# Six modulation units moved from TensorE to GpSimd, and the second block's first norm and latent products done tile by tile

## The reference, cut to what matters

```python
# first block
mod = (silu(c) @ w_mod[l] + b_mod[l])[:, None, :]              # 1024 x 6144
sh1, sc1, gt1, sh2, sc2, gt2 = jnp.split(mod, N_MOD, axis=-1)
h = layer_norm(x) * (1.0 + sc1) + sh1
y = hybrid_mixer(h, w_in, conv_w, ...)          # conv + chunked SSD, forgetting attention
x = layer_norm(ALPHA * x + (1.0 + gt1) * y, ln1_g, ln1_b)
h = layer_norm(x) * (1.0 + sc2) + sh2
y = hierarchical_moe(h, ...)                    # 16 experts, two of one group of four
x = layer_norm(ALPHA * x + (1.0 + gt2) * y, ln2_g, ln2_b)
# second block
mod = (silu(c_2) @ w_ada[l] + b_ada[l])[:, None, :]            # six more rows
h = rmsnorm(x, g_norm_mix) * (1.0 + sc1) + sh1
c_q, c_kv, k_pe, dil, gates = jnp.split(h @ w_in_2, ...)       # latents: the first 704 columns
o_a = mla_attention(...); o_b = three dilated attentions
x = x + gt1 * ((g_a * o_a + g_b * o_b) @ w_out)
x = x + gt2 * expert_choice_ffn(rmsnorm(x) * (1.0 + sc2) + sh2, ...)
```

## Time and profile before

| | |
|---|---|
| median of 3 runs | 2143.76 us (2142.66 to 2144.46) |
| the profiled execution | 2143.5 us |
| its span, first to last instruction | 2141.7 us |
| mean granted TensorE clock | 0.873 of full |
| busy: PE, PEld, DVE, ACT, POOL | 1616.5, 829.8, 419.9, 283.1, 60.3 us |
| read from HBM | 661.86 MB |

### The profile page before, as it was taken

The page is one execution under the profiler, slowest core; times in us unless marked ns, Lnnn a source line. Parts: engine busy times, 40 slices in busy tenths (PEclk is TensorE's granted clock), DMA queues, the critical chain, the costliest instruction groups (busy, mean ns, idle before and its releaser), DMA issues.

```text
span 2141.7 us, 19636 instructions
## 1 busy us (share of the span) xinstructions
PE 1616.5 (75%) x8021; PEld 829.8 (39%) x8021; DVE 419.9 (20%) x912; ACT 283.1 (13%) x632; POOL 60.3 (3%) x79
## 2 busy tenths in 40 slices
PE   6999999899998999999999644664365545545545
PEld 3774654344442677686644311311131111211111
DVE  5521642432213122121325200000000000000001
ACT  6211222110001222121233100000000000000000
POOL 2000000000000100111100000000000000000000
PEclk9999999989999999999999767877787777777777
DMA  9999332849997642344527499999999999999996
GB/s 354 336 365 348 105 100 79 343 164 421 427 428 293 225 176 100 133 143 138 175 75 287 197 428 428 428 427 429 427 428 427 428 427 428 427 428 428 427 428 265
DMA packets 104236, 670.53 MB, mean 313 GB/s; under 512 B 8227, under 2 KB 10984, under 8 KB 71120
## 3 DMA queue, kind: packets, MB, share of 16 engines
q1 hardware_dynamic: 100000, 657.63, 75.4%
q0 software_dynamic: 3712, 11.11, 1.6%
q10 hardware_dynamic: 432, 0.49, 0.1%
HBM read 661.86 MB, written 7.34 MB: 312 GB/s over the span
## 4 chain that ended last, share of the span: by engine, by line
PE 62%; DMA 32%; DVE 3%; ACT 2%; SPq 1%; issue 1%; DVEq 0%; ACTq 0%
PE psum L1099 14%; PE psum L1088 12%; DMA ring<-in_w_up 11%; DMA ring<-in_w_down 11%; PE psum L1695 10%; DMA ring<-in_w_gate 9%; PE psum L1434 5%; PE psum L1466 3%; PE psum L1351 2%; PE psum L1402 2%; PE psum L1054 2%; PE psum L1180 1%; PE psum L1473 1%; PE psum L1562 1%; SPq L786 1%
## 5 line engine op out<-in xcount | busy, mean ns | idle before, releaser
L1695 PE MATMUL psum<-work,prob 128*32 128x512 f32 x1024 | 290.9, 732 | 162.3 <-DMA ring<-in_w_up 87.2
L1695 PE MATMUL psum<-ring,prob 128*32 128x512 f32 x1024 | 291.0, 732 | 143.1 <-DMA work<-in_w_up 83.1
L1099 PE MATMUL psum<-ring,hT 128*128 128x512 f32 x672 | 306.3, 602 | 5.0 <-ACT hT L181 4.2
L1088 PE MATMUL psum<-hT,ring 128*128 128x256 f32 x1152 | 270.5, 381 | 1.6 <-ACT probT L181 0.8
L1088 PEld LDWEIGHTS psum<-hT,ring 128*128 128x128 f32 x1152 | 210.7, 190 | 36.2 <-issue 8.0
L1695 PE MATMUL psum<-work,hT 128*32 128x512 f32 x512 | 143.0, 721 | 82.7 <-DMA ring<-in_w_down 82.7
L1695 PE MATMUL psum<-ring,hT 128*32 128x512 f32 x512 | 143.0, 721 | 54.4 <-DMA work<-in_w_down 51.0
L1099 PEld LDWEIGHTS psum<-ring,hT 128*128 128x128 f32 x672 | 123.8, 193 | 138.6 <-issue 132.6
L1695 PEld LDWEIGHTS psum<-work,prob 128*32 128x32 f32 x1024 | 70.8, 131 | 267.2 <-issue 267.2
L1695 PEld LDWEIGHTS psum<-ring,prob 128*32 128x32 f32 x1024 | 71.0, 131 | 248.3 <-issue 247.3
L181 ACT ACTIVATE work<-psum 128x512 f32<-128x512 f32 (+2 forms) x99 | 57.0, 576 | 650.2 <-PE psum L1709 313.9
(11 more groups left out here) (334 smaller groups left out, 1430.0 us busy)
## 6 DMA issues: line engine op xcount, KB each, us to landing
work<-in_w_up SPq DMA_DIRECT2D x40, 2048.0 KB, 20.1
ring<-in_w_up SPq DMA_DIRECT2D x40, 2048.0 KB, 19.9
ring<-in_w_gate SPq DMA_DIRECT2D x38, 2048.0 KB, 18.8
work<-in_w_gate SPq DMA_DIRECT2D x38, 2048.0 KB, 19.6
work<-in_w_down SPq DMA_DIRECT2D x38, 2048.0 KB, 20.2
ring<-in_w_in SPq DMA_DIRECT2D x72, 1024.0 KB, 7.5
ring<-in_w_down SPq DMA_DIRECT2D x34, 2048.0 KB, 21.1
ring<-in_w_mod SPq DMA_DIRECT2D x24, 1024.0 KB, 12.5
```

Source lines behind the costliest of these rows:

```text
L1088: mm = pe.matmul(o[:, wide(j * S, S)], w[:, ch], actT[:, c, :], start=(c == 0), stop=(c == KC - 1))
L1099: mm = pe.matmul(o, lhs, w, start=(c == 0), stop=(c == KC - 1))
L1695: mm = pe.matmul(o[wide(i * CAP2, CAP2), :], lhs(chunks_per * piece + c, i), R.slot(l + i, (chunks_per, width))[:, c, wide(b * BANK, BANK) ...
```

## The change

Units 2 to 7 are no longer products on TensorE. POOL fetches their weights itself, 512 KB at a time (one channel chunk of one unit, 128x1024), multiplies each with the condition's value of that partition (tensor_scalar) and adds it to a running sum (tensor_tensor): 8 parts for each of 6 units. TensorE then only adds over the partitions, with a stationary block that has one column of ones (add_partitions: two products of 64 columns). The sums of unit 2 and 3 are taken behind the last xbc chunk and behind v, that of unit 4 in the SSD, those of 5, 6 and 7 in steps 2, 8 and 14 of the forgetting attention. Units 8 and 9 are still products; they stand behind z chunk 0 and z chunk 1.

Units 2 and 3 are spread after the first merge product and unit 4 after the last, and ACT takes them from PSUM. The register with the overflow flag is loaded before the rounds of experts. In the second block, each tile's first norm, modulation, transposes and latent products follow one another tile by tile; unit 8 is spread between the latents' transposes and q, and q_peT goes ahead of the second half of dil_q0's first chunk. One buffer of POOL's parts lies in h, three small tiles lose their own memory, and the constants get 32 columns.

```diff
-        IN_UNITS = dict(xbc=(2, 3, 4, 5), q=(6,), k=(7,), v=(8,), z=(9,))
+        IN_UNITS = dict(xbc={3: 2}, q={}, k={}, v={0: 3}, z={0: 8, 1: 9})
+        FOX_SUMS = {2: 5, 8: 6, 14: 7}
...
+        BESIDE_H = 3
+        part_places = [mod[:, 0, :], mod[:, 1, :], mod[:, 2, :], h[:, 0, :], h[:, 1, :], params[:, 1, :]]
+            streams = (2, 3, 4) if i < BESIDE_H else (2, 5)
...
+            def fetch_part(n):
+                u, c, b = unit_parts[n]
+                if c == 0 and u >= POOL_UNITS[2]:
+                    pool.wait_ge(*done(job(f"unit{u - 2}")))
+                if b == 5 and all(place != 5 for _, _, place in unit_parts[:n]):
+                    pool.wait_ge(bias_stored[BIAS_STAGES - 1], BIAS_GROUPS // BIAS_STAGES * BIAS_STORES)
+                if c and step.last:
+                    pool.wait_ge(*step.last)
+                src = (w_mod, w_ada)[u // 6].rearrange("(p c) n -> p c n", c=KC)[:, c, wide(u % 6 * D, D)]
+                pool.dma_start(part_places[b], src).then_inc(part_in[b], 16)
+
+            def add_part(n):
+                u, c, b = unit_parts[n]
+                pool.wait_ge(part_in[b], 16 * len([m for m in range(n + 1) if unit_parts[m][2] == b]))
+                step(nc.gpsimd.tensor_scalar, part_places[b], part_places[b], cact[:, u // 6, c:c + 1], None, ALU.mult)
+                if c:
+                    step(nc.gpsimd.tensor_tensor, unit_sum(u), part_places[b], unit_sum(u), ALU.add, signals=unit_summed(u) if c == KC - 1 else None)
+
+            def place_free(n, added):
+                u, c, b = unit_parts[n]
+                before = [m for m in range(n) if unit_parts[m][2] == b]
+                return n <= added + 6 and (c == 0 or not before or before[-1] <= added)
+
+            pool.wait_ge(signal("cact_ready"), 1)
+            pool.wait_ge(signal("hT_high"), KC // 2)
+            fetched = 0
+            for n in range(-1, len(unit_parts)):
+                if n >= 0:
+                    add_part(n)
+                while fetched < len(unit_parts) and place_free(fetched, n):
+                    fetch_part(fetched)
+                    fetched += 1
...
+            def add_partitions(u):
+                o = begin(job(f"unit{u}"))
+                pe.wait_ge(*unit_summed(u))
+                for n in range(2):
+                    mm = pe.matmul(o[wide(64 * n, 64), :], one_column_at(u), unit_sum(u)[:, wide(n * BANK, BANK)], start=True, stop=True)
+                units_done.append(u)
+                end(mm)
...
-            spread(2, 3, 4)
...
+            more_tokens = overflow_flag(pe)
...
-            with more_tokens(pe):
+            with pe.If(more_tokens > 0):
...
-            transpose_tokens("h3T", h, "h3_ready")
-            for k in range(4):
-                pe.wait_ge(*emptied(job("h3T", k)))
...
+            for t in range(TT):
+                transpose_tokens("h3T", h, "h3_ready", (t,))
+                if t:
+                    latent(1, 0)
+                for half in range(2):
+                    pe.wait_ge(*emptied(job("h3T", 2 * t + half)))
+                latent(0, t)
+            latent(1, 1)
...
+            spread(8)
             for k in range(4):
                 pe.wait_ge(*emptied(job("latT", k)))
...
-            in_one(channel_job("dil_q0", 0, 1, hT))
-            spread(8)
             for t in range(TT):
                 pe.wait_ge(signal("q_pe_ready"), t + 1)
...
+            in_one(channel_job("dil_q0", 0, 1, hT))
...
-                if ct % 4 == 3:
+                if ct % 4 == 3 and ct // 4 in IN_UNITS["xbc"]:
                     add_row(IN_UNITS["xbc"][ct // 4])
...
+            dve.wait_ge(*unit_summed(POOL_UNITS[BESIDE_H - 1]))
             for m in range(2 * TT):
                 assemble(m)
...
-            rms_modulated(0, "h3_ready")
+            dve.wait_ge(signal("params_in"), 64)
+            for t in range(TT):
+                norm_stats(6 + t, t, y_sum)
+                normalize(x, 6 + t, t, params[:, 0, :], params[:, 1, :], (signal("x_b1_ready"), t + 1), y_sum)
+                rms_modulated(0, "h3_ready", (t,))
```

## The result

The changed kernel takes 2183.78 us (median of 4 runs, 2180.33 to 2183.96) where the kernel before takes 2143.21: a ratio of 1.019, interval 1.0176 to 1.0205. It is 1.9% slower, clear of the noise, and the time lies above the range. The profiled execution has a span of 2178.5 us and a mean granted clock of 0.866.

A forecast was written before the change was run, and what follows sets the result against it. TensorE was taken to set the pace through the first block's experts, transfers from about 1200 us. Terms came to about 0 up to the experts, then -4.1 to -3.9: 2143.5 - 4.1 = 2139.4, stated as 2139 us, range 2124 to 2158.

The forecast's parts named there:

- six sums: TensorE's sums over partitions for the six units, two products each, 0.45 us a sum; +2.7 us in all.
- masks: First block's convolution: VectorE, contending with POOL, delivers masks for the last two bias products late; +8 us (0.5 to 15).
- dtf: A sum on TensorE that waits for VectorE's convolution in the first block; the prediction had no term for it.
- angle chain: Ahead of the cumulative sums: with unit 9 behind the last z chunk, VectorE's steps are no longer hidden; +4.2 us.
- SSD, with the way to x_end: SSD: VectorE slowed beside POOL, +1.5 us (0 to 6); way to x_end not covered by the spread, +0.5.
- attention, besides its sums: Forgetting attention: POOL has 13 parts to do after unit 5's sum, so TensorE waits; +4 us (0 to 20).
- second block: Second block: -4.8 us for the tile-by-tile stage, +0.9 for the new order of q_peT and unit 8.
- POOL's part: One tensor_scalar (taken as 1.1 us), one tensor_tensor and one load issue on POOL; 4.2 us a part (4.0 to 5.5).
- POOL's part is 5.5 us: Rival, chance 0.18: slow tensor_scalar or late loads make the attention wait 20 us instead of 4; 2155 us.
- The hold-up of VectorE: POOL's instructions stall VectorE's two-SBUF-input instructions from about 53 us; charged 8 us at the convolution, 1.5 in the SSD.
- every second turn is POOL's: Rival, chance 0.22: POOL alternates with VectorE, 15.3 us instead of 8 at the convolution, 4 instead of 1.5 in SSD; 2149.
- Tile by tile: Second block's first norm to latent products, done per tile: first latent product starts earlier; -4.8 us (-2 to -8).

The follow-up runs named there:

- second: The kernel before with all of the change except the six units moved to POOL; 2137.2 us, ratio 0.9974.
- cheap_mul: The changed kernel with POOL's multiplication replaced by a copy of the tile to itself; its whole time, 2880.9 us, can't be used because tokens went into the overflow loop.
- no_arith: The changed kernel with POOL's multiplications and additions on one column instead of 1024, loads and waits kept; 2131.35 us, ratio 0.9948.
- angle: The changed kernel with unit 8 behind k and unit 9 ahead of the last z chunk; 2176.8 us, ratio 1.0143.
- late_start: The changed kernel with POOL beginning its units only when VectorE has made the last mask; 2177.9 us, ratio 1.0162.
- three_late: The kernel before with early overflow flag, tile-by-tile stage, and only units 5 to 7 on POOL, behind the convolution; ratio 1.0001.
- tiles: The kernel before with only the early overflow flag and the second block's tile-by-tile first norm, transposes and latent products; 2135.0 us, ratio 0.9967.
- mended: The changed kernel with multiplication as broadcast tensor_tensor, POOL starting behind the last mask, and unit 9 ahead of the last z chunk; 2184.6 us, ratio 1.0189.

## Why the prediction was wrong, step by step

| term | predicted | measured |
|---|---|---|
| six units off TensorE | -21.4 | -21.4 |
| six sums | +2.7 | +7.4 (five of 1.08, one of 1.97) |
| masks | +8 | +15.5 (wait 13.4, slow clock 2.1) |
| dtf | none | +8.9 (7.4 and 1.5) |
| angle chain | +4.2 | +13.8 (wait 11.45, slow clock 2.4) |
| SSD, with the way to x_end | +2.0 (1.5 and 0.5) | +4 |
| attention, besides its sums | +4 | +16.6 (wait 14.4, the rest 2.2) |
| transposes ahead of w_o, behind ACT's copies | +0.3 | +1.5 (wait 2.4 for 1.0) |
| second block | -3.9 | -5.6 (`second`) |

**POOL's part** is the step that failed first. I said that the tensor_scalar "lies between a memset of that size, 0.95, and the product with two inputs, 2.36", and took 1.1; it is 2.87, above both ends. The upper bound had no ground: the nearest row was of another operation. The rival *POOL's part is 5.5 us* was right in mechanism and sign, and still too small (6.2). With its 5.5 us the attention was to wait 20. It waits only 14.4 with 6.2, because the count of parts was off as well: when TensorE adds unit 5, at 305.05, POOL has 11 parts left and not 13. `cheap_mul` shows the attention's wait gone at the assumed rate.

**The hold-up of VectorE** was foreseen and undersized. The rival *every second turn is POOL's* was the nearest to the truth, and its price for the masks (15.3) was met within 0.2. That is luck in part. The working gives 12.3 and 0.5 for it and nowhere the rest, and it assumes parts of 4.2 us; with parts of 4.2 us `cheap_mul` has a wait of 17.4 there. I chose the middle between two mechanisms (8) where the evidence, one pair in the earlier trace rows, showed a full stop. The worse error was to follow it to the masks only: the other twelve tiles, up to 6.2 us each, end at 154.5 instead of 132.5, and the sum of dtf waits; and the angle chain, "one answer: DVE's order can't change", was costed at its old durations while POOL is busy beside it. `no_arith` confirms the 4.2 for it without POOL (4.3). The sum counted nothing for dtf, and no reason was given for that.

The Trainium skill's rule in "SBUF — State Buffer", "Who interferes with whom", was cited for the rival. The trace bears out its full block beside POOL's tensor_tensor (the 2.53 us above). Beside POOL's tensor_scalar it doesn't: at 116.72 a VectorE instruction with two SBUF inputs begins ahead of POOL's tensor_scalar and ends after 1.51 us, 1.5 us ahead of that one's end, and neither the lone 0.49 us nor a full block gives that. The same section says that VectorE's tensor_scalar can enter a mode in which it uses both ports and then contends, too, and the trace agrees: 1.23 us for 0.41.

**The sums**: I counted two rows of 0.22 for a sum; the trace has four rows to it (x24 for six), as one product in float32 gives two. By that count the 256 rows are 128 products of 0.44, which I overlooked; a sum by itself also shows its latency.

**SSD**: in the changed kernel TensorE has no wait for x_end; POOL stood still from 241 to 260 us, while x_end was made. Its waits are at the end of the SSD, 1.6 and 0.9 us for VectorE, and the clock is low behind them. Where POOL works while x_end is made and the spread is gone, "the way to x_end: +0.5" was too small: 3.5 us in `angle` and `late_start`, 3.4 in `three_late`. With the spread gone and POOL's arithmetic out (`no_arith`) there is no wait.

**Right**: the units' 3.57 each; POOL held by TensorE in the SSD; the new order of q_peT (+0.9, and +1.2 read). The addition up to the experts has the 0.3 of ACT twice, which doesn't matter here. **Tile by tile**, -4.8, is -7.1 (4.7 to 9.2 by the interval) as a time. By the trace of `tiles`, unit 10 starts 7.35 us behind the start of the last experts' products (8.68 before), and the queries' first products 54.0 (58.8 before), which is the -4.8; the second scores are 3.2 us nearer. From there the profile gains another 3 us up to the end, for which I have no cause.

The measured column adds up to +40.7, and so does the ratio of 1.019, but the profiled execution itself is only 36.8 us longer than that of before. So the agreement to the tenth is chance.

The steps that failed, in short: a price of 1.1 us for an instruction that takes 2.87, and a hold-up of VectorE that was charged at the masks alone and at 8 us, where it cost 15.5 there, 8.9 at dtf and 9.6 more than reckoned at the angle chain.

## What to carry to other kernels

Work that is moved to GpSimd is paid for by VectorE, in turns: while both keep asking, about one VectorE instruction with SBUF operands passed for each tensor_tensor of GpSimd and each issue, and two for each tensor_scalar, however short its own time. So count VectorE's instructions in the stretch, not its busy time, and follow the delay to every consumer, not to the first. An operation that no row shows has no upper bound in rows of other operations: measure it alone before the sum rests on it, and look whether the next engine (here perhaps the transfers) has room for what is taken off the bound one.

## What the hardware showed that I had not expected

- GpSimd's tensor_scalar of 128x1024 takes 2.77 us with a number and 2.85 with a column, its copy 1.04, and the same multiplication as a tensor_tensor with the column broadcast 1.90.
- A cheaper form on GpSimd made VectorE slower: means of 1.21 us per scalar_tensor_tensor beside parts of 2.87 + 2.35 (`late_start`), and 1.79 beside 1.90 + 2.35 (`mended`). During the tensor_scalar a VectorE instruction gets in between, during the tensor_tensor none does.
- Cut into quarters, GpSimd's multiplication costs 0.65 us (a quarter of the whole would be 0.47) or, as a tensor_scalar, 0.95 (0.71), and VectorE's mean falls to 0.78. The tensor_tensor of 128x256 costs 0.74 with VectorE idle, 0.75 beside it.
- VectorE's reads from PSUM are not held up: the copy of 128x512 takes 0.75 us a piece in the changed kernel at 81.96 (1.49 for two), beside a tensor_scalar of POOL, as before.
